# Hybrid attention/DeltaNet block with a 32-expert MoE: at each change of expert, the down of the old expert's last block is put ahead of the new expert's first gate_up

## Chip, cores and metric

The kernel runs on one core of one Trainium2 chip. The metric is device time of one execution in microseconds. The kernel before took 1259.33 us, the median of three runs (1258.27 to 1259.81).

## The reference

The function is one layer over 512 tokens of width 1024, all in float32. A first part (input projection, sliding-window attention, a gated DeltaNet, output projection) gives `h`; it is not touched here. Then comes the mixture of experts: each token goes to 4 of 32 experts, and each expert runs on its own tokens only.

```python
def clamped_swiglu_expert(xb, w_gu, b_gu, w_down, b_down):
    gu = xb @ w_gu + b_gu                      # (rows, 1024) @ (1024, 2048)
    gate = jnp.minimum(gu[:, :D_FF], SWIGLU_LIMIT)
    up = jnp.clip(gu[:, D_FF:], -SWIGLU_LIMIT, SWIGLU_LIMIT)
    act = (up + 1.0) * (gate * jax.nn.sigmoid(gate * SWIGLU_ALPHA))
    return act @ w_down + b_down               # (rows, 1024) @ (1024, 1024)
# y[token] += gate_of_row * clamped_swiglu_expert(row of the token); h = h + y
```

The weights of one expert are 8 MiB (`w_gu`) and 4 MiB (`w_down`).

## The kernel before

**Blocks.** The first part ends some 320 us into the span; everything after it is one loop over blocks. A block is 32 rows (token and gate) of one expert. With these inputs there are 81 blocks, numbered through over all experts. `LASTB[e]` holds the number of the last block of the e-th expert in the order of work; the expert with the fewest tokens' blocks comes last. The activations of a block are the stationary operand (32 columns), the weights stream through. The four column groups of the PE array work on four quarters of the output at once.

**PE** (L1102 to L1165). `gate_up(i)` multiplies block i, held transposed in XT, with the eight k slices of the gate/up weights into bank GPS; it waits for XT (`xt_ready`), for the bank (`gu_evac`), and at the first block of an expert for each of the four 2 MiB parts of the weights (`gu_in`). `down(i)` multiplies the activations of block i, held transposed in AT, with the down weights into DPS, half a PSUM bank. It waits for AT (`at_ready`), for DPS to be read by the block before (`yt_ready`), and for the two parts of the down weights. In program order the PE does gate_up(i), then down(i - 1), and so on; this holds inside an expert (`more_blocks`, L1134) and, before the change, at a change of expert too (`expert`, L1142). Each f32 matmul shows as two records in the trace, so a gate_up or a down has 64.

**DVE** (L1546 to L1632). `activate(i)` adds the bias to GPS (L1554), clamps (L1556, L1558), copies the next block's gathered tokens into XT (`x_turn`, L1549), multiplies with the sigmoid and the gate value (L1562, L1564), and transposes the result into AT (L1572). Before that transpose it spreads the down bias of block i - 1 into SIG (`spread_dn_bias`, L1580) and loads 16 token numbers into registers. After it, `y_evac(i - 1)` adds gate times down bias to DPS (L1585), transposes it into YTV (L1590) and adds 16 of its 32 columns onto the tokens in ACC (L1594). At a change of expert `spread_gu_bias` (L1438) spreads the new gate/up bias into BGU ahead of `activate`. For the last expert (`turn_first`) the spread and token loads come behind the transpose.

**ACT** (L669 to L697) does, in turn, the sigmoid of block i and the gathering of block i + 2 into XG. **POOL** (L424 to L454) does the other half of the gathering, of block i + 3 (L428), and then the other 16 adds of block i (L438).

**SP** (L340 to L350) issues the loads on one queue. There are two weight buffers; `reload` loads expert e + 2 into the buffer of expert e: first the four gate/up parts, each when the last gate_up of expert e has read it (L240); then it waits until the down bias of that expert's last block has been spread (`bdn_spread`, L344), loads the new biases (L231, L235) and then the two down parts, which wait for the last down of expert e (L246).

Of the kernel before, what the change touches and what calls it, by code (L numbers as in the profile page):

```python
# [25 lines left out]
HALF = BT // 2  # L26
# [13 lines left out]
def hybrid_block(nc, x, norm_mix_w, w_in, qn_w, kn_w, sinks, conv_w, a_log, dt_bias, out_norm_w, w_out,  # L40
                 norm_ffn_w, router_w, router_b, w_gu, b_gu, w_dn, b_dn, out):
    ctx = ExitStack()
    with ctx:
# [3 lines left out]
        def S_(name):  # L47
            if name not in sems:
                sems[name] = ctx.enter_context(nc.semaphore(name))
            return sems[name]  # L50
# [165 lines left out]
        def within(i, most, why):  # L216
            return i if isinstance(i, int) else nc.s_assert_within(i, 0, most, skip_runtime_bounds_check_because=why)
        def tokens_of(engine, i, first, count):
            at = within(i, MAXB, "no routing gives more than MAXB blocks, and one is gathered behind them")
            row = TOK[i:i + 1, first:first + count] if isinstance(i, int) else bass.at_runtime_partition(TOK[0:1, first:first + count], at)  # L220
            return nc.values_load_multi_w_load_instructions(row, engines=[engine], min_val=0, max_val=COLS - 1 if first < BT else S - 1,
                                                            skip_runtime_bounds_check_because="a token, or a column behind the last one")[1]
# [479 lines left out]
        def _(pe):  # L702
# [133 lines left out]
            for i in range(CHU + 2):  # L836
# [3 lines left out]
                if 2 <= i < NCH + 2:  # L840
# [7 lines left out]
                    v = AQ[0:k, (n - 1) // 2 if n else 0, 640:768] if n % 2 or n == 0 else AVS[:, n // 2 - 1, :]  # L848
# [253 lines left out]
            def gate_up(i, p, rnd, first_of_expert, first):  # L1102
                pe.wait_ge(S_("xt_ready"), i + 1)
                if not first:
                    pe.wait_ge(S_("gu_evac"), i)
                for k in range(KD):
                    if first_of_expert and k % 2 == 0:
                        pe.wait_ge(S_(f"gu_in{p}{k // 2}"), rnd)
                    for j in range(4):
                        rhs = GUW[p][:, k, :].rearrange("p (g n) -> p g n", g=2)[:, :, j * QW:(j + 1) * QW]  # L1110
                        last = pe.matmul(GPS[32 * j:32 * j + 32, :].rearrange("p (g n) -> p g n", g=2),  # L1111
                                         XT[:, 32 * k:32 * k + 32], rhs,
                                         start=(k == 0), stop=(k == KD - 1), tile_position=(0, 32 * j), skip_group_check=True)
                    if k % 2:
                        last.then_inc(S_(f"gu_read{k // 2}" if k < KD - 1 else "gu_ps"), 1)
                    if first and k in between:
                        between[k]()
            def down(i, p, rnd, to=DPS):
                pe.wait_ge(S_("at_ready"), i + 1)
                if to is DPS:  # L1120
                    pe.wait_ge(S_("yt_ready"), i + 1)
                pe.wait_ge(S_(f"dn_in{p}0"), rnd)
                for k in range(KD):
                    if k == KD // 2:
                        pe.wait_ge(S_(f"dn_in{p}1"), rnd)
                    for j in range(4):
                        rhs = DNW[p][:, k, :].rearrange("p (c q x) -> p q c x", c=KD, q=4)[:, j]
                        last = pe.matmul(to[32 * j:32 * j + 32, :].rearrange("p (c x) -> p c x", c=KD),  # L1128
                                         AT[:, 32 * k:32 * k + 32], rhs,
                                         start=(k == 0), stop=(k == KD - 1), tile_position=(0, 32 * j), skip_group_check=True)  # L1130
                    if k == KD // 2 - 1:
                        last.then_inc(S_("dn_read"), 1)
                last.then_inc(S_("d_ps"), 1)
            def more_blocks(e, p, before, rnd, last):  # L1134
# [5 lines left out]
                        down(i - 1, p, rnd)  # L1140
                return last
            def expert(e, p, before, rnd, prnd, last=None):  # L1142
                gate_up(before + 1, p, rnd, True, False)
                down(before, 1 - p, prnd)
                return more_blocks(e, p, before, rnd, last)
            gate_up(0, 0, 16, True, True)
            pe.wait_ge(S_("rows4"), 1)
# [30 lines left out]
        def _(v):  # L1178
# [255 lines left out]
            def spread_gu_bias(e, p, rnd):  # L1434
                v.wait_ge(S_(f"bias_in{p}"), rnd * 6)
                v.sem_inc(S_("passed"), 1)
                for q in range(4):
                    ins = v.stream_shuffle(BGU[:, QH * q:QH * q + QH], RAWP[p], [q] * 32)  # L1438
                ins.then_inc(S_("bias_spread"), 1)
                v.wait_ge(S_("bias_spread"), e + 1)  # L1440
# [105 lines left out]
            def x_turn(i):  # L1546
                v.wait_ge(S_("a_gathered"), i)
                v.wait_ge(S_("g_gathered"), i)
                v.tensor_copy(XT[:, :], XG[:, :]).then_inc(S_("xt_ready"), 1)  # L1549
            def activate(i, p, first, before_p=None, turn_first=False):  # L1550
                v.wait_ge(S_("gu_ps"), i + 1)
                if not first:
                    v.wait_ge(S_("at_ready"), i)
                tt(GU, GPS.rearrange("p (g n) -> p g n", g=2), BGU[:, :].rearrange("p (g n) -> p g n", g=2), ALU.add).then_inc(S_("gu_evac"), 1)  # L1554
                v.wait_ge(S_("gu_evac"), i + 1)
                ts(GATED, GATED, LIMIT, None, ALU.min).then_inc(S_("gate_ready"), 1)  # L1556
                x_turn(i + 1)
                ts(UP, UP, LIMIT, -LIMIT, ALU.min, ALU.max)  # L1558
                v.wait_ge(S_("sig_ready"), i + 1)
                if first:  # L1560
                    v.wait_ge(S_("lists_done"), 1)
                stt(out=SIG[:, :], in0=SIG[:, :], scalar=gate_of(i), in1=GATED, op0=ALU.mult, op1=ALU.mult).then_inc(S_("glu"), 1)  # L1562
                v.wait_ge(S_("glu"), i + 1)
                stt(out=GATED, in0=UP, scalar=1.0, in1=SIG[:, :], op0=ALU.add, op1=ALU.mult).then_inc(S_("act_ready"), 1)  # L1564
                v.wait_ge(S_("act_ready"), i + 1)
                def prepare():
                    spread_dn_bias(i - 1, before_p)
                    return tokens_of(v.engine, i - 1, 0, HALF)
                if not first and not turn_first:
                    toks = prepare()  # L1570
                v.wait_ge(S_("d_ps"), i + 1)
                v.transpose(ATV, ACTV).then_inc(S_("at_ready"), 1)  # L1572
                if turn_first:
                    toks = prepare()
                if not first:
                    y_evac(i - 1, toks)
            def spread_dn_bias(i, p):
                v.sem_inc(S_("passed"), 1)
                for h in range(2):
                    ins = v.stream_shuffle(SIG[:, QH * h:QH * h + QH], RAWP[p], [4 + h] * 32)  # L1580
                ins.then_inc(S_("bdn_spread"), 1)
                v.wait_ge(S_("bdn_spread"), i + 1)
            def y_evac(i, toks, start=DPS):
                v.wait_ge(S_("d_ps"), i + 2)
                stt(out=YG, in0=SIG[:, :], scalar=gate_of(i), in1=start, op0=ALU.mult, op1=ALU.add).then_inc(S_("y_ready"), 1)  # L1585
                v.wait_ge(S_("y_ready"), i + 1)
                if not (isinstance(i, int) and i == 0):
                    v.wait_ge(S_("g_added"), i)
                    v.wait_ge(S_("v_added"), i)
                v.transpose(YTV, YG.rearrange("p (k m) -> p k m", k=KD)).then_inc(S_("yt_ready"), 1)  # L1590
                v.wait_ge(S_("yt_ready"), i + 2)
                for m in range(len(toks)):
                    col = ACCV[:, :, bass.ds(toks[m], 1)]
                    ins = tt(col, col, YTV[:, :, m:m + 1], ALU.add)  # L1594
                ins.then_inc(S_("v_added"), 1)
# [9 lines left out]
            with v.If(last > 0):  # L1605
                activate(1, 0, False, 0)
# [2 lines left out]
                    activate(i, 0, False, 0)  # L1609
            def expert(e, p, before, rnd, last=None):  # L1610
                turn_first = last is not None
                spread_gu_bias(e, p, rnd)
                activate(before + 1, p, False, 1 - p, turn_first)
                if last is None:
                    last = v.value_load(LASTB[0:1, bass.ds(e, 1)], min_val=0, max_val=MAXB - 1)
                with v.If(last > before + 1):
                    with v.Fori(before + 2, last + 1) as i:
                        activate(i, p, False, p, turn_first)
                return last
# [31 lines left out]
```

## Time and profile before

| | |
|---|---|
| median of three runs | 1259.33 us |
| the profiled execution's own time | 1258.68 us |
| its span, first to last instruction | 1257.0 us |
| mean granted TensorE clock | 0.980 |
| PE matmul busy | 1180.9 us (94%) |
| DVE / ACT / POOL busy | 725.0 / 566.8 / 446.6 us |
| DMA | 427.71 MB, mean 340 GB/s |

Times are from one execution. A busy PE is a PE with a matmul under way by the profile, whose ends are modelled: two records that touch may overlap by some 0.2 us, so durations of gate_ups and downs are best read as the distance from start to start. The chain of work that ended last has PE with 65% of the span and DMA with 24%. `L1111` is the matmul of gate_up, `L1128` that of down.

### The profile page before, as it was taken

What the parts mean: (1) busy time and instruction counts of PE and PEld (TensorE: products, weight loads), DVE (VectorE), ACT (ScalarE), POOL (GpSimd) and SP (SyncE); (2) the same over time, 40 slices, a digit from 0 to 9 for tenths busy, and PEclk for the clock granted to TensorE, in tenths of its full rate; (3) what the DMA queues carried; (4) which work ended last, traced back from release to release, by engine and by line L of the source; (5) the groups of instructions that cost most, each with busy time, mean ns of one, the idle gap of its engine ahead of it and who ended that gap; (6) DMA issues with size and microseconds to landing.
All of it is one profiled execution on the core that took longest, in us unless ns stands there. A gap on an engine that the chain in (4) does not pass through costs nothing.

```text
span 1257.0 us, 46595 instructions
## 1 busy us (share of the span) xinstructions
PE 1180.9 (94%) x12074; PEld 554.9 (44%) x12075; DVE 725.0 (58%) x3048; ACT 566.8 (45%) x4249; POOL 446.6 (36%) x2632
## 2 busy tenths in 40 slices
PE   6999999999899998989998999999999778999996
PEld 5875456766444432323342444444444222334333
DVE  2237766555666664646565666666666444666564
ACT  3135666324354553535454555555555333555450
POOL 0000003000255553545454455555555333555451
PEclk9999999999999998999999999999999898999998
DMA  5141116347999999999999999999999999999995
GB/s 189 39 137 61 40 35 179 94 167 325 370 376 410 427 426 426 427 425 428 426 425 424 426 424 410 407 411 406 403 406 431 425 425 427 428 426 421 428 426 223
DMA packets 53768, 427.71 MB, mean 340 GB/s; under 512 B 13232, under 2 KB 25824, under 8 KB 29152
## 3 DMA queue, kind: packets, MB, share of 16 engines
q1 hardware_dynamic: 51552, 427.07, 82.5%
q10 hardware_dynamic: 2176, 0.13, 0.1%
q8 instruction: 22, 0.36, 0.1%
q14 instruction: 18, 0.15, 0.0%
HBM read 424.63 MB, written 2.36 MB: 340 GB/s over the span
## 4 chain that ended last, share of the span: by engine, by line
PE 65%; DMA 24%; DVE 5%; SPq 2%; issue 2%; ACT 1%; DVEq 0%; ACTq 0%; POOL 0%
PE PS L1111 30%; DMA W<-in_expert_w_gate_up 23%; PE PS L704 15%; PE PS L1128 14%; PE HTP L704 3%; SPq L231 1%; SPq L241 0%; DMA W<-in_norm_mix_w 0%; SPq L235 0%; PE HTP L880 0%; PE HTP L714 0%; DVE W L1192 0%; DVE ACC L1594 0%; PE HTP L1175 0%; DVE SIG L1580 0%
## 5 line engine op out<-in xcount | busy, mean ns | idle before, releaser
L1111 PE MATMUL PS<-W,XT 128*32 128x512 f32 x5184 | 594.5, 608 | 53.3 <-DMA W<-in_expert_w_gate_up 47.0
L1111 PEld LDWEIGHTS PS<-W,XT 128*32 128x32 f32 x5184 | 167.5, 111 | 426.3 <-issue 345.0
L673 ACT ACTIVATE XG<-HTP 128x6 f32 x2592 | 259.6, 181 | 155.3 <-issue 155.3
L428 POOL COPY XG<-HTS 128x2 f32 x1296 | 200.7, 213 | 298.3 <-DVE XT L1549 292.7
L438 POOL TENSOR_TENSOR ACC<-ACC 128x8 f32 x1292 | 226.9, 218 | 198.6 <-DVE ACC L1590 198.6
L1128 PE MATMUL PS<-W,AT 128*32 128x256 f32 x5120 | 293.5, 381 | 0.0
L1128 PEld LDWEIGHTS PS<-W,AT 128*32 128x32 f32 x5120 | 169.1, 111 | 149.2 <-issue 54.6
L704 PE MATMUL PS<-W 128*128 128x512 f32 (+3 forms) x680 | 219.3, 477 | 3.0 <-ACT W L625 1.1
L683 ACT ACTIVATE SIG<-GU 128x256 f32<-128x256 f32 x81 | 33.9, 418 | 339.1 <-DVE GU L1556 338.8
L1594 DVE TENSOR_TENSOR ACC<-ACC 128x8 f32 x1300 | 161.6, 187 | 13.8 <-issue 1.3
L704 PEld LDWEIGHTS PS<-W 128*128 128x128 f32 (+1 forms) x680 | 124.0, 191 | 76.8 <-issue 64.8
L676 ACT ACTIVATE XG<-HTS 128x2 f32 x1280 | 136.5, 192 | 0.2 <-issue 0.2
L1554 DVE TENSOR_TENSOR GU<-PS,BGU 128x512 f32<-128x512 f32 x81 | 56.0, 692 | 129.2 <-PE PS L1111 128.8
L1572 DVE STREAM_TRANSPOSE AT<-GU 128x256 f32<-128x256 f32 x81 | 53.1, 655 | 105.5 <-issue 97.9
L384 POOL TENSOR_TENSOR W<-W 128x512 f32<-128x512 f32 x4 | 5.1, 1266 | 190.8 <-ACT W L526 190.8
L1438 DVE LOAD_MASK_SELECT BGU<-RAW x128 | 1.8, 14 | 90.7 <-DMA RAW<-in_expert_b_down 73.9
L1562 DVE SCALAR_TENSOR_TENSOR SIG<-SIG,LATE,GU 128x256 f32<-128x256 f32 x81 | 39.3, 485 | 14.6 <-ACT SIG L683 14.6
L704 PE MATMUL HTP<-W 128*128 128x128 f32 (+6 forms) x368 | 43.5, 288 | 0.7 <-DMA W<-inv_scratch 0.6
L704 PEld LDWEIGHTS HTP<-W 128*128 128x128 f32 (+3 forms) x368 | 37.7, 186 | 12.7 <-issue 12.5
L1580 DVE STREAM_SHUFFLE SIG<-RAW 128x128 f32<-128x128 f32 x162 | 41.3, 300 | 0.7
L1590 DVE STREAM_TRANSPOSE ACC<-PS 128x256 f32<-128x256 f32 x81 | 36.4, 450 | 2.8
L1585 DVE SCALAR_TENSOR_TENSOR PS<-SIG,LATE,PS 128x256 f32<-128x256 f32 x80 | 35.9, 448 | 1.8 <-issue 1.8
(280 smaller groups left out, 630.9 us busy)
## 6 DMA issues: line engine op xcount, KB each, us to landing
W<-in_expert_w_gate_up SPq DMA_DIRECT2D x128, 2048.0 KB, 25.6
W<-in_expert_w_down SPq DMA_DIRECT2D x64, 2048.0 KB, 22.0
W<-in_w_in SPq DMA_DIRECT2D x10, 1024.0 KB, 5.9
W<-in_x SPq DMA_DIRECT2D x8, 512.0 KB, 11.1
W<-in_w_out SPq DMA_DIRECT2D x2, 1024.0 KB, 9.7
W<-in_w_out SPq DMA_DIRECT2D x1, 2048.0 KB, 8.2
RAW<-in_expert_b_gate_up SPq DMA_DIRECT2D x128, 2.0 KB
out<-W SPq DMA_DIRECT2D x8, 256.0 KB, 2.8
```

Of the source, the lines that this page charges most:

```text
L428: ins = g.tensor_copy(XGK[:, KP:KD, HALF + m:HALF + m + 1], HTS[:, :, bass.ds(toks[m], 1)])
L438: ins = g.tensor_tensor(col, col, YTV[:, :, m:m + 1], ALU.add)
L673: ins = a.activation(XGK[:, 0:KP, m:m + 1], HTP[:, :, bass.ds(toks[m], 1)], ACT.Copy)
L676: ins = a.activation(XGK[:, KP:KD, m:m + 1], HTS[:, :, bass.ds(toks[m], 1)], ACT.Copy)
L704: return pe.matmul(o, l, r, start=st, stop=sp_)
L1111: last = pe.matmul(GPS[32 * j:32 * j + 32, :].rearrange("p (g n) -> p g n", g=2), XT[:, 32 * k:32 * k + 32], rhs, start=(k == 0), stop=(k ...
L1128: last = pe.matmul(to[32 * j:32 * j + 32, :].rearrange("p (c x) -> p c x", c=KD), AT[:, 32 * k:32 * k + 32], rhs, start=(k == 0), stop=(k ...
L1554: tt(GU, GPS.rearrange("p (g n) -> p g n", g=2), BGU[:, :].rearrange("p (g n) -> p g n", g=2), ALU.add).then_inc(S_("gu_evac"), 1)
L1562: stt(out=SIG[:, :], in0=SIG[:, :], scalar=gate_of(i), in1=GATED, op0=ALU.mult, op1=ALU.mult).then_inc(S_("glu"), 1)
L1572: v.transpose(ATV, ACTV).then_inc(S_("at_ready"), 1)
L1580: ins = v.stream_shuffle(SIG[:, QH * h:QH * h + QH], RAWP[p], [4 + h] * 32)
L1594: ins = tt(col, col, YTV[:, :, m:m + 1], ALU.add)
```

## The change

On PE, `expert` calls down(before) ahead of gate_up(before + 1). On the DVE, `expert` does the spread of the old down bias, the token loads and y_evac of block `before` ahead of the new gate/up bias and of activate(before + 1), which gets `added=True` and leaves all three out. This holds for all 31 changes of expert, the last one included. Inside an expert nothing changes. No instruction is added to or taken from the work; ACT, POOL and SP keep their programs.

```diff
             def expert(e, p, before, rnd, prnd, last=None):
+                down(before, 1 - p, prnd)
                 gate_up(before + 1, p, rnd, True, False)
-                down(before, 1 - p, prnd)
                 return more_blocks(e, p, before, rnd, last)
...
-            def activate(i, p, first, before_p=None, turn_first=False):
+            def activate(i, p, first, before_p=None, turn_first=False, added=False):
...
                 def prepare():
                     spread_dn_bias(i - 1, before_p)
                     return tokens_of(v.engine, i - 1, 0, HALF)
-                if not first and not turn_first:
+                if not first and not turn_first and not added:
                     toks = prepare()
                 v.wait_ge(S_("d_ps"), i + 1)
                 v.transpose(ATV, ACTV).then_inc(S_("at_ready"), 1)
-                if turn_first:
+                if turn_first and not added:
                     toks = prepare()
-                if not first:
+                if not first and not added:
                     y_evac(i - 1, toks)
...
             def expert(e, p, before, rnd, last=None):
                 turn_first = last is not None
+                spread_dn_bias(before, 1 - p)
+                y_evac(before, tokens_of(v.engine, before, 0, HALF))
                 spread_gu_bias(e, p, rnd)
-                activate(before + 1, p, False, 1 - p, turn_first)
+                activate(before + 1, p, False, 1 - p, turn_first, True)
```

## Rows read from the trace of the kernel before

**Rows 1.** The page, part 2: busy tenths of PE and of the DMA engines, 40 slices.
```profile
PE   6999999999899998989998999999999778999996
...
DMA  5141116347999999999999999999999999999995
```

**Rows 2.** The page, part 5: groups; count | busy us, mean ns | idle before, releaser.
```profile
L1111 PE MATMUL PS<-W,XT 128*32 128x512 f32 x5184 | 594.5, 608 | 53.3 <-DMA W<-in_expert_w_gate_up 47.0
...
L1128 PE MATMUL PS<-W,AT 128*32 128x256 f32 x5120 | 293.5, 381 | 0.0
```

**Rows 3.** Waits of PE: who waited for whom, us in total, times, longest.
```profile
PE PS L1111 <- DMA W<-in_expert_w_gate_up: 47.0, 21, 3.1
...
PE PS L1111 <- issue: 3.6, 15, 0.6
```

**Rows 4.** Stretches: length, busy us (records) of PE, PEld, DVE, ACT, POOL; clock, DMA, GB/s.
```profile
332.00:470.00 138.00, 136.62 (x1680) 55.97 (x1680) 86.30 (x405) 71.19 (x665) 68.44 (x416) 1.00 0.96 404
...
693.00:955.00 262.00, 261.16 (x3236) 107.69 (x3232) 166.02 (x793) 131.46 (x1226) 132.47 (x800) 1.00 0.98 412
955.00:1057.00 102.00, 82.19 (x896) 28.42 (x892) 47.70 (x235) 36.70 (x344) 37.00 (x225) 0.90 1.01 427
```

**Rows 5.** Timeline, 742 to 770: start us, us, engine, line [idle before <-releaser].
```profile
748.68 7.05 PE L1111 MATMUL PS<-W,XT 128*32 128x512 f32 x64
...
755.55 3.64 PE L1128 MATMUL PS<-W,AT 128*32 128x256 f32 x64
...
759.42 7.07 PE L1111 MATMUL PS<-W,XT 128*32 128x512 f32 x64 [0.23 <-issue]
...
760.32 0.65 DVE L1572 STREAM_TRANSPOSE AT<-GU 128x256 f32<-128x256 f32 x1 [1.29 <-issue]
...
761.38 0.45 DVE L1590 STREAM_TRANSPOSE ACC<-PS 128x256 f32<-128x256 f32 x1
...
765.28 0.01 DVE L1438 LOAD_MASK_SELECT BGU<-RAW  x1 [1.35 <-issue]
...
766.30 3.64 PE L1128 MATMUL PS<-W,AT 128*32 128x256 f32 x64
...
767.58 0.29 DVE L1549 COPY XT<-XG 128x256 f32<-128x256 f32 x1
```

**Rows 6.** Timeline of SP: the closest two gate_up reloads.
```profile
933.04 1.90 SPq L241 DMA_DIRECT2D W<-in_expert_w_gate_up  x4
...
953.87 3.73 SPq L241 DMA_DIRECT2D W<-in_expert_w_gate_up  x4
```

**Rows 7.** Timeline, the start of gate_up 1.
```profile
332.64 0.29 DVE L1549 COPY XT<-XG 128x256 f32<-128x256 f32 x1 [0.38 <-ACT XG L673]
...
332.99 7.07 PE L1111 MATMUL PS<-W,XT 128*32 128x512 f32 x64 [1.58 <-DVE XT L1549]
```

**Rows 8.** Timeline, the last expert.
```profile
1220.00 3.64 PE L1111 MATMUL PS<-W,XT 128*32 128x512 f32 x32 [0.60 <-issue]
...
1233.85 3.63 PE L1128 MATMUL PS<-W,AT 128*32 128x256 f32 x64
...
1236.32 0.43 DVE L1564 SCALAR_TENSOR_TENSOR GU<-GU,SIG 128x256 f32<-128x256 f32 x1
...
1239.57 3.66 PE L1128 MATMUL HTP<-W,AT 128*32 128x256 f32 x64
...
1244.47 0.49 DVE L1585 SCALAR_TENSOR_TENSOR PS<-SIG,LATE,HTP 128x256 f32<-128x256 f32 x1 [0.22 <-DVE SIG L1580]
```

**Rows 9.** Timeline of PE: work behind three long waits.
```profile
595.45 3.48 PE L1111 MATMUL PS<-W,XT 128*32 128x512 f32 x16 [2.56 <-DMA W<-in_expert_w_gate_up]
...
685.12 1.92 PE L1111 MATMUL PS<-W,XT 128*32 128x512 f32 x16 [2.78 <-DMA W<-in_expert_w_gate_up]
...
1171.06 2.69 PE L1111 MATMUL PS<-W,XT 128*32 128x512 f32 x16 [2.63 <-DMA W<-in_expert_w_gate_up]
1173.51 4.62 PE L1128 MATMUL PS<-W,AT 128*32 128x256 f32 x64
```

## The prediction

> **What bounds the kernel now.** The slices of the page come first. From slice 11 on PE and the DMA engines are both mostly full (9s and a few 7s and 8s) [rows 1]. So the question is not which of the two is busier but whose waits end last. The groups of the page give the amount: 5184 matmuls are 81 gate_ups of 64 records, 5120 are 80 downs; the 81st down writes another bank [rows 2]. The waits of PE say that over the expert loop it stood 47.0 us for gate_up weights, in 21 waits, and nearly nothing else [rows 3]. The table of stretches shows how this alternates: between 693 and 955 PE is busy 261 of 262 us and the DMA moves 412 GB/s; between 955 and 1057 PE is busy 82 of 102 and the DMA is at its 427 [rows 4]. PE and DMA are thus nearly balanced: without its weight waits PE has little to give away.
>
> **The unit of the sum.** In a full stretch a gate_up goes from one start to the next down in 6.87 us (748.68 to 755.55) and a down takes 3.45 us (its record shows a modelled end 0.2 later); where a pair of experts starts, 0.42 us comes on top (759.42 less 755.55 is 3.87), 15 times [rows 3, 5]. SP's gate_up reloads are released by the last gate_up of an expert. The closest two are 20.8 us apart, two blocks (20.64), so every expert but the last has two or more blocks; the last has one, block 80, whose gate_up starts at 1220.00 [rows 6, 8]. There are 31 changes of expert.
>
> From the start of gate_up 1 (332.99) to that of the last down (1239.57) pass 906.6 us [rows 7, 8]. In it are 80 x 6.87 = 549.6, 80 x 3.45 = 276.0, 15 x 0.42 = 6.3 and 5.7 from the last gate_up's end to the last down (1233.85 to 1239.57): 837.6. The other 69.0 are the 47.0 of weight waits and 22.0, which I put down to matmuls at half clock behind them.
>
> **What moves, part by part.** Call b the last block of the old expert and G the end of its gate_up.
>
> *Down ahead of gate_up, on PE.* Now down(b-1) covers the DVE chain of b, and gate_up(b+1) covers the rest, so down(b) never waits. Afterwards down(b) comes straight behind down(b-1), and it needs two things of the DVE: the turned activations (L1572) and the y of b-1 turned out of DPS (L1590). Both stand in one unchanged piece of code. For G = 755.55 that L1590 ends at 761.83; down(b-1) ends at G + 3.45 = 759.00 [rows 5]. The last DVE write to the PE start takes 0.06 us (L1549 ends at 332.93, the gate_up that waits for it starts at 332.99) [rows 7]. So PE stands 761.89 - 759.00 = **2.89 us, 31 times: 89.6**. The 0.42 of a new pair now lies ahead of this down, inside its wait: 6.3 less. Of it 1.29 are the token loads ahead of the turn (the idle "issue" before L1572) [rows 5]; the change drops them only from the first block of an expert, and that one is never the last here.
>
> *Second wait.* The down used to stand between gate_up(b+1) and gate_up(b+2). Now gate_up(b+2) follows at once and needs L1554 (the bank) and L1549 (XT) of b+1. At a first gate_up of an expert L1549 ends at 767.87, 1.57 after the gate_up's end at 766.30; with the 0.06 this is **1.63 us, 30 times (the last expert has one block): 48.9** [rows 5]. The one place of the trace with this order, gate_up 0 to gate_up 1, shows 1.58 [rows 7].
>
> *Last expert.* Its down waited 5.72 us after its gate_up, for down(before), spread and turn. Now L1564 ends 2.90 after the gate_up, the turn takes 0.65 and follows at once: 3.65 with the hand-overs. And the last y_evac (L1585 at 1244.47) no longer stands behind 16 adds of the block before: 1.1 less [rows 8].
>
> *On the DVE*, what goes ahead of activate(b+1) is the spread, 16 token loads, L1585, L1590, 16 adds, then the four shuffles of the gate_up bias. The adds of b-1 end 1.35 before the next work at 765.28 (G + 9.7); 0.6 for the spread, 1.3 for the loads, 3.1 for L1585 to L1594 (L1572 ends at 760.97, the adds at 763.93) and 1.1 for four shuffles (twice the spread's two) give G + 15.8. gate_up(b+1) ends at G + 3.45 + 2.89 + 3.45 + 6.87 = G + 16.7 [rows 5]. The cover is 0.9 us; I take 0. If it is gone, it is L1554 and with it gate_up(b+2) that come late, us for us.
>
> *POOL and ACT.* POOL's 16 adds of b stay behind gather(b+3), which waits for XT of activate(b+1); they take as long as now, and nobody needs them until y_evac(b+1), a gate_up and a down later. ACT's gathers keep their releases. Nothing.
>
> *SP.* It waits for the down spread before it issues the biases and the down weights. The spread ends 3.5 after the gate_up of its activate (L1572 less the loads is 759.03), so at G + 3.45 + 6.87 + 3.5 = G + 13.8 [rows 5]; it will end at G + 10.2, and down(b) ends 4 us earlier: down weights leave about 3.5 us sooner. That mends the 404 and 412 GB/s of two stretches: 138 x (1 - 404/427) + 262 x (1 - 412/427) = 16.6 us of DMA time at most [rows 4]. It is worth time only if the DMA still bounds. An expert's six parts of 2048 KB take 12.58 MB / 427 = 29.5 us of the DMA; PE took 81/32 x 10.32 = 26.1 and will take 30.6. PE becomes the bound, and its 47.0 of waits with the 22.0 behind them go.
>
> Without the clock: 549.6 + 276.0 + 89.6 + 48.9 + 3.65 = 967.8 against 906.6, and 1.1 less at the end: **+60 us**.
>
> **The clock.** This is the disputed term. Ten waits of PE lie between 2.56 and 3.15 us. Behind eight of them the granted clock fell to half (1.2 GHz of 2.4): behind 2.56 us of idleness the quarter of a gate_up took 3.48 instead of 1.92, behind 2.63 us it took 2.69 and the down 4.62 instead of 3.64; behind those at 685.12 (2.78) and 1016.78 it stayed [rows 9]. The 2.89 stalls are of this kind, those of 1.63 are not: no wait that short, alone, was followed by a fall. One fall costs 1.56 to 1.75 us. The bounds are none (0) and all (31 x 1.75 = 54); I take the share seen, 8 of 10, so 25 x 1.65 = **41 us**. The Trainium skill, "TensorE: Matmul & The Clock Gate", section "Why this matters for your kernels", advises no idle gaps above about 3 us between bursts. By that rule a stall of 2.9 leaves the clock whole, and the sum would end at +60; the rows at 595 and 1171 speak against it.
>
> Sum: +60 + 41 = +101 on the profiled run's 1258.68: **1360 us**. That run lies 0.65 under the median of 1259.33, which I leave out.
>
> **Rivals.**
> 1. *The clock holds.* +60: 1319 us. For it: PE is fully busy before and after each stall, while several of the eight falls had a second wait near. Against: 595 and 1171. 0.20.
> 2. *The DVE comes late at the first gate_up of an expert.* The 0.9 us of cover rests on one 1.35 us of loop overhead and a chain without a gap. If it is 1.9 longer, 1 us x 30 comes on top: 1390 us. 0.12.
> 3. *Faster.* The stalls fall where PE waits for weights anyway, and the DMA stays the bound, now without gaps. The point that decides: PE has 69.0 to lose over 31 changes, 2.2 us each; below this the end is set by the DMA, 16.6 us earlier at best: 1242 us. It needs down(b) ready almost as down(b-1) ends. Against it, L1590 alone ends 2.83 after that. 0.02.
> 4. *Nothing.* The stalls use up just the waits, or the order in effect does not change: 1259 us. The code's waits exclude nearly all of it. 0.02.
>
> My forecast (PE-bound, clock lost at most stalls) has 0.64. All slower cases make 0.96. A difference under 0.2% (2.5 us) could not be told from none here.
>
> **Range.** Low end: rival 1 with stalls 0.2 and 0.1 shorter (9 us): 1310. High end: all 31 falls at 1.75 (+13) and 0.4 us of DVE lateness at each change (+13): 1387. Left out are most of rival 2 and the last two.
>
> **What would show it.** In the changed profile, L1128 after a change of expert should wait for DVE L1590, 31 times about 2.7 to 2.9 us; L1111 30 times about 1.5 for L1549; waits for gate_up weights should be nearly gone and the DMA's GB/s lower. Falls of the clock should be counted near 25. I am wrong if PE still waits over 20 us for weights, if the stall at down is under 2 us, or if L1554 starts more than 0.5 after the end of its gate_up.

## The result

The changed kernel took 1368.07 us (median of four runs, 1366.11 to 1371.11), the kernel before 1258.8 (four runs, 1258.13 to 1259.81). The ratio is 1.086, with a 95% interval of 1.0836 to 1.0884: 109 us slower. The forecast was 1360 us in a range of 1310 to 1387. The profiled execution of the changed kernel took 1369.76 us, its span is 1368.0.

### The profile after

First the page of the changed kernel: the head, the busy tenths of PE and of the DMA engines, and the two groups of matmuls.

```profile
span 1368.0 us, 46670 instructions
...
PE   7999999998889788888888988898888888888886
...
DMA  5121045079898999989879677777899999979981
...
L1111 PE MATMUL PS<-W,XT 128*32 128x512 f32 x5184 | 572.7, 593 | 44.6 <-DVE XT L1549 43.4
L1128 PE MATMUL PS<-W,AT 128*32 128x256 f32 x5120 | 336.7, 422 | 88.4 <-DVE ACC L1590 46.7
```

Against [rows 1, 2] the counts are the same; it is the idle time ahead of them that changed its owner. Ahead of gate_ups stood the DMA with 47.0 us, now it is the DVE with 43.4; ahead of downs stood nothing, now 88.4. The 9s of the DMA have given way to 6s to 8s in the long experts. gate_up records are shorter than before (593 ns against 608) and down records longer (422 against 381): half clock used to fall on gate_ups behind weight waits, now it falls on downs.

The waits of PE, the counterpart of [rows 3] (who waited for whom, us in total, times, longest):

```profile
PE PS L1128 <- DVE ACC L1590: 46.7, 16, 3.1
PE PS L1111 <- DVE XT L1549: 43.4, 31, 1.6
PE PS L1128 <- DVE AT L1572: 41.6, 15, 3.0
...
PE HTP L1128 <- DVE AT L1572: 2.6, 1, 2.6
```

That is the new loop: 31 stalls at a down and 31 at a gate_up, of which one (gate_up 1) was there before. There is no row for weights any more.

The stretches of [rows 4] (length, busy us with records of PE, PEld, DVE, ACT, POOL, then clock, DMA share, GB/s):

```profile
332.00:470.00 138.00, 119.68 (x1361) 47.98 (x1357) 70.71 (x336) 60.10 (x563) 55.53 (x341) 0.95 0.91 382
...
693.00:955.00 262.00, 232.42 (x2719) 94.90 (x2712) 141.48 (x682) 112.83 (x1059) 112.17 (x681) 0.96 0.81 339
955.00:1057.00 102.00, 86.44 (x1028) 36.34 (x1024) 54.10 (x263) 42.20 (x395) 43.27 (x264) 0.95 0.95 401
```

Between 693 and 955 the clock was 1.00 and is 0.96, and the DMA went from 412 to 339 GB/s. PE waits for no weights in any of them: PE, with its stalls behind the DVE, sets the pace.

One change of expert on PE, the counterpart of [rows 5] (start us, us, engine, line, tiles, idle before and its releaser):

```profile
770.90 3.64 PE L1128 MATMUL PS<-W,AT 128*32 128x256 f32 x64
777.28 5.35 PE L1128 MATMUL PS<-W,AT 128*32 128x256 f32 x64 [2.74 <-DVE AT L1572]
782.41 7.08 PE L1111 MATMUL PS<-W,XT 128*32 128x512 f32 x64
...
503.01 3.66 PE L1128 MATMUL PS<-W,AT 128*32 128x256 f32 x64 [2.76 <-DVE AT L1572]
```

down(b-1) starts at 770.90 and would be done at 774.35; down(b) starts at 777.28, 2.93 later, and takes 5.35 us in place of 3.66. The row at 503.01 is one of the four of 31 where it kept its 3.66 after a stall of the same length. The granted clock in both (columns as above) says why:

```profile
777.60:780.80 3.20, 3.20 (x36) 1.97 (x32) 2.17 (x19) 1.61 (x16) 2.63 (x15) 0.50 1.02 435
503.10:506.40 3.30, 3.30 (x64) 2.42 (x67) 2.42 (x20) 1.83 (x19) 2.87 (x16) 1.00 1.04 442
```

And the DVE beside the change at 777.28:

```profile
775.68 0.64 DVE L1572 STREAM_TRANSPOSE AT<-GU 128x256 f32<-128x256 f32 x1 [1.28 <-issue]
...
776.73 0.45 DVE L1590 STREAM_TRANSPOSE ACC<-PS 128x256 f32<-128x256 f32 x1
...
782.78 0.49 DVE L1585 SCALAR_TENSOR_TENSOR PS<-SIG,LATE,PS 128x256 f32<-128x256 f32 x1 [2.86 <-PE PS L1128]
...
786.68 0.30 DVE L1438 STREAM_SHUFFLE BGU<-RAW 128x128 f32<-128x128 f32 x1
...
789.60 0.69 DVE L1554 TENSOR_TENSOR GU<-PS,BGU 128x512 f32<-128x512 f32 x1 [2.62 <-issue]
```

L1590 ends at 777.18 and the down starts 0.10 later. (The profile names L1572 as releaser at half of the changes; the start follows L1590 by 0.10 at these too. At the 15 changes where a new pair of experts starts it follows L1590 by 0.23 to 0.30.) The first L1554 of the new expert starts 0.32 after its gate_up's end at 789.28, having been free for 2.6 us: the DVE is not late.

### The profile page after: what moved, and what is told of

The parts are those of the page before. It is cut to its first block, busy times and chain, and to the rows that moved or that the text cites. A ratio compares the mean times of both kernels' runs of the same rounds, so it can differ in the third digit from the quotient of the medians.

```text
span 1368.0 us, 46670 instructions
## 1 busy us (share of the span) xinstructions
PE 1212.7 (89%) x12074; PEld 584.3 (43%) x12075; DVE 727.1 (53%) x3048; ACT 566.6 (41%) x4249; POOL 443.5 (32%) x2632
## 4 chain that ended last, share of the span: by engine, by line
PE 69%; DVE 14%; issue 9%; DVEq 3%; ACT 2%; DMA 1%; ACTq 0%; SPq 0%; POOL 0%
PE PS L1111 34%; PE PS L1128 16%; PE PS L704 13%; DVE GU L1554 3%; PE HTP L704 3%; DVEq L221 3%; DVE SIG L1580 1%; DVE BGU L1438 1%; DVE SIG L1562 1%; DVE GU L1564 1%; ACT SIG L683 1%; DVE AT L1572 1%; DVE GU L1556 1%; DVE XT L1549 1%; DVE ACC L1590 1%
## 5 line engine op out<-in xcount | busy, mean ns | idle before, releaser
L1111 PE MATMUL PS<-W,XT 128*32 128x512 f32 x5184 | 572.7, 593 | 44.6 <-DVE XT L1549 43.4
L1128 PE MATMUL PS<-W,AT 128*32 128x256 f32 x5120 | 336.7, 422 | 88.4 <-DVE ACC L1590 46.7
L1111 PEld LDWEIGHTS PS<-W,XT 128*32 128x32 f32 x5184 | 172.4, 110 | 411.5 <-issue 331.6
L1128 PEld LDWEIGHTS PS<-W,AT 128*32 128x32 f32 x5120 | 191.4, 121 | 245.6 <-issue 118.2
L438 POOL TENSOR_TENSOR ACC<-ACC 128x8 f32 x1292 | 223.8, 217 | 147.3 <-DVE ACC L1590 127.4
L1554 DVE TENSOR_TENSOR GU<-PS,BGU 128x512 f32<-128x512 f32 x81 | 56.0, 692 | 275.0 <-PE PS L1111 199.1
L1572 DVE STREAM_TRANSPOSE AT<-GU 128x256 f32<-128x256 f32 x81 | 52.4, 647 | 66.3 <-issue 64.0
L1585 DVE SCALAR_TENSOR_TENSOR PS<-SIG,LATE,PS 128x256 f32<-128x256 f32 x80 | 37.1, 464 | 68.1 <-PE PS L1128 65.1
L704 PE MATMUL HTP<-W 128*128 128x128 f32 (+6 forms) x368 | 43.4, 288 | 0.8 <-DMA W<-inv_scratch 0.7
L1590 DVE STREAM_TRANSPOSE ACC<-PS 128x256 f32<-128x256 f32 x81 | 36.4, 450 | 2.8
L1564 DVE SCALAR_TENSOR_TENSOR GU<-GU,SIG 128x256 f32<-128x256 f32 x81 | 34.4, 425 | 2.8
```

The source lines that it names most:

```text
L438: ins = g.tensor_tensor(col, col, YTV[:, :, m:m + 1], ALU.add)
L704: return pe.matmul(o, l, r, start=st, stop=sp_)
```

## The experiments

They ran in two groups, each on one chip beside the kernel before. Its median was 1258.85 in the first (early loads, filled stall, 16 of 31 changes, the queue) and 1259.83 in the second (the control, the transposes, the XT copy first, both edits); between the groups that 1.0 us is to be kept in mind.

### Shorter DVE chain at the stall

```diff
+                early = not first and not turn_first and not added
+                if early:
+                    toks = tokens_of(v.engine, i - 1, 0, HALF)
                 v.wait_ge(S_("gu_ps"), i + 1)
...
-                if not first and not turn_first and not added:
-                    toks = prepare()
+                if early:
+                    spread_dn_bias(i - 1, before_p)
```

> The changed kernel, with the 16 token loads of the DVE's y_evac taken ahead of its wait for the gate_up, so that the chain from the end of a gate_up to L1572 and L1590 is 1.29 us shorter. My theory (the down stall is this DVE chain, and a stall near 3 us costs a fall of the clock besides): the stall at the down goes from 3.0 to 1.7 us (31 x 1.29 = 40 us), the 27 falls vanish (27 x 1.69 = 46 us), and the weight waits come back a little, since an expert now takes the PE about as long as the DMA: 1283 to 1292 us. Rival A (the falls follow the change of order, not the length of the stall): 1328 us, with some 27 falls. Rival B (down(b) waits for something else, the bank or the DMA): no change, 1368 us.

Measured: 1295.87 us, ratio 1.0275 (1.0225 to 1.0324). PE's waits, and one change:

```profile
PE PS L1128 <- DVE ACC L1593: 29.7, 16, 1.9
PE PS L1128 <- DVE AT L1575: 26.0, 15, 1.7
...
PE PS L1111 <- DMA W<-in_expert_w_gate_up: 1.1, 1, 1.1
```

```profile
739.06 3.64 PE L1128 MATMUL PS<-W,AT 128*32 128x256 f32 x64
744.43 3.66 PE L1128 MATMUL PS<-W,AT 128*32 128x256 f32 x64 [1.73 <-DVE AT L1575]
```

The stalls shrank and with them every slow down went: all 31 took 3.66, and the mean clock of the run is 0.997. That kills both rivals. My own number was 4 us low at its upper end, since the stall is 1.92 (744.43 less 739.06 and 3.45), and 2.05 where a new pair of experts starts, not 1.7. The DVE row that shows the new limit:

```profile
742.84 0.64 DVE L1575 STREAM_TRANSPOSE AT<-GU 128x256 f32<-128x256 f32 x1 [0.27 <-PE PS L1128]
```

The transpose (L1575 here is L1572) now waits for down(b-1) to be done with AT, of which there is one. Once the chain is short, the order itself holds the stall: turn into AT, L1585, L1590, one after the other behind down(b-1). A second AT and a second DPS were not tried, nor a down that waits for L1585 alone: DPS and the YG that L1590 reads share a PSUM bank. The Trainium skill, "PSUM — Partial Sum Buffer", section "PSUM bank collisions raise a hardware error", rules out a PE write beside a DVE read of one bank; no run here shows it.

### The same loads early in the old order

The same edit on the kernel before, as a control.

> The kernel before with the same early token loads as in the run e1_loads_early. My theory (in the old order the DVE chain is covered by the gate_up that stands ahead of the down, so its length is worth nothing): 1257 to 1261 us, no difference from before. Rival (the chain limits the kernel in the old order too, and part of what that run gained has nothing to do with the new order): up to 1.0 us for each of 80 blocks less, bounded by the DMA at about 1245 us.

Measured: 1260.12 us, ratio 1.0005 (0.9995 to 1.0015). The chain is worth nothing in the old order; what it cost in the new one is the price of the new order.

### The stall filled with work

```diff
             def expert(e, p, before, rnd, prnd, last=None):
+                pe.wait_ge(S_("gu_evac"), before + 1)
+                for _ in range(9):
+                    mm(GPS[:, 0:P], ident[:, :], ident[:, :], True, True)
                 down(before, 1 - p, prnd)
```

> The changed kernel, with nine 128x128 f32 matmuls of the identity by itself into the free gate_up bank inside the stall ahead of the down at each change of expert (about 2 us of work of no use). My theory: the stalls themselves stay, the PE is no longer idle in them, the clock stays whole at all 31, and the time falls by 27 x 1.69 = 46 us to 1322 us. Rival (the slow downs come from something else than the idle time before them, such as cold reads of the new operand, or these matmuls do not count): 1366 to 1370 us, with the down behind the stall still at 5.35 us.

Measured: 1327.37 us, ratio 1.0551 (1.0487 to 1.0615), one change of it:

```profile
752.44 3.64 PE L1129 MATMUL PS<-W,AT 128*32 128x256 f32 x64
756.01 2.27 PE L705 MATMUL PS<-ident 128*128 128x128 f32 x18
758.82 3.66 PE L1129 MATMUL PS<-W,AT 128*32 128x256 f32 x64 [0.54 <-issue]
762.27 7.08 PE L1112 MATMUL PS<-W,XT 128*32 128x512 f32 x64
```

From start to start the two downs are 6.38 us apart, in the changed kernel 6.38 (770.90 to 777.28): the stall is as long as it was, only not idle, and the down behind it takes 3.66. All 31 did, and over all 31 the stalls sum to 94.2 us, against 94.1. So the clock alone was worth 45.4 us in the loop. The run was 41 us faster and not 45 (and 5 slower than I expected), because the last change took some back. Here is the very last down, first in the changed kernel, then in this run:

```profile
1351.70 3.66 PE L1128 MATMUL HTP<-W,AT 128*32 128x256 f32 x64 [2.58 <-DVE AT L1572]
...
1307.66 5.35 PE L1129 MATMUL HTP<-W,AT 128*32 128x256 f32 x64 [3.87 <-DVE AT L1576]
```

In this run it waited 1.3 us longer and was itself slow, which is another 1.7.

With 18 transposes in place of the nine matmuls:

> As the run e2_filled_stall, but the stall is filled by 18 transposes of the identity in place of the nine matmuls, the same 2 us of PE work. Theory 1 (a transpose keeps the clock as a matmul does): 1326 to 1328 us, one fall or none in the loop. Theory 2 (transposes do not count as work for the clock, as a page of the Trainium skill has it, TensorE: Matmul & The Clock Gate, Part 4): some 27 falls, 1366 to 1370 us.

Measured: 1326.98 us, ratio 1.0536 (1.0518 to 1.0554), mean clock 0.997. For the clock a transpose was as good as a matmul here.

### The new order at 16 of 31 changes

```diff
             def expert(e, p, before, rnd, prnd, last=None):
-                down(before, 1 - p, prnd)
+                if p:
+                    down(before, 1 - p, prnd)
                 gate_up(before + 1, p, rnd, True, False)
+                if not p:
+                    down(before, 1 - p, prnd)
```

The DVE's part likewise.

> The order is changed only at the 16 changes into odd experts; at the 15 into even ones the kernel is as before. Theory 1, mine (PE had 69 us of waits for weights and of slow matmuls behind them to lose before any stall costs time): 16 stalls of 3.1 + 1.6 us with 1.7 of clock are 102 us, of which a good half goes into waits that vanish; 1285 to 1296 us. Theory 2 (each change of order costs its share, the effect is linear): half of 109, 1313 us. Theory 3 (the DMA hides all of it): 1259 us.

Measured: 1289.41 us, ratio 1.0229 (1.018 to 1.0277). 

```profile
PE PS L1128 <- DVE ACC L1593: 46.5, 16, 3.1
PE PS L1111 <- DVE XT L1552: 22.6, 16, 1.6
...
PE PS L1111 <- DMA W<-in_expert_w_gate_up: 5.0, 2, 2.5
```

Half of the changes cost 31 us, 28% of the 109 of all. Slow downs followed 15 of the 16 stalls. The first stalls eat the waits for weights (47.0 have become 5.0), and the other 15 changes cost 79 us. That is theory 1, and it refutes an equal price per change.

### The second stall

```diff
+                if added:
+                    x_turn(i + 1)
                 tt(GU, GPS.rearrange("p (g n) -> p g n", g=2), BGU[:, :]...
...
-                x_turn(i + 1)
+                if not added:
+                    x_turn(i + 1)
```

> The changed kernel, but at the first block of an expert the DVE copies XT (L1549) ahead of the bias add (L1554), so that both are done 0.3 us sooner after the gate_up. My theory (the second stall, ahead of the next gate_up, is bound by these two): it goes from 1.59 to about 1.3 us at 30 changes, and the time falls by 9 us to 1359 us. Rival (what the second stall costs is made up elsewhere, or it is bound by the gathers of ACT and POOL): 1366 to 1370 us.

Measured: 1355.36 us, ratio 1.0766 (1.0731 to 1.0801).

```profile
PE PS L1111 <- DVE GU L1556: 34.7, 30, 1.2
```

The second stall went from 43.4 less one 1.6 to 34.7, 7 us, and it does lie on the path. The rest of the 12.7 us goes with the clock: 22 of the downs behind a stall were slow in this profile, 27 in the one of the changed kernel, and five at 1.68 are 8 us; the last expert, whose down waited 1.5 us longer here and was slow, takes some of that back. Whether the shorter second stall has a part in the fewer falls stays open. Both edits together:

> Both edits, the early token loads and the XT copy first, on the changed kernel: as near as the new order gets without new buffers. The down stall stays at the 1.9 us of the run e1_loads_early (L1572 now waits for down(b-1) to be done with AT, and the down for L1590), the second at 1.3: 9 us less than that run's 1296, of which the weight waits take back 0 to 4, so 1287 to 1291 us. Rival (the DMA already bounds that run): 1294 to 1297 us.

Measured: 1291.55 us, ratio 1.0258 (1.0241 to 1.0275), 4 us under the run with the early loads alone, where I had expected 9 less 0 to 4, and half a microsecond above the expected range. The second stall shrank by 0.24 us, not by 0.3 (34.8 us for 30 of them in this profile), and weight waits of 2.5 took a part back. It stays 32 us behind the kernel before. No version with the new order came nearer to the old one than 30 us.

### The down part of the queue alone

```diff
                 gu_part(e, p, range(4), through)
+                dn_part(e, p, [0], through)
                 sp.wait_ge(S_("bdn_spread"), through)
                 gu_bias(e, p)
                 dn_bias(e, p)
-                dn_part(e, p, range(2), through)
+                dn_part(e, p, [1], through)
```

on the kernel before.

> The kernel before, but SP loads the first down part as soon as the last down of the old expert has read it, ahead of its wait for the spread of the down bias; biases and the second part behind. This does alone what the change did for the DMA queue on the side: down weights leave earlier. My theory: where PE sets the pace the queue ran dry for a few us per expert, 16.6 us in all at most, and the DMA sets the end: 1250 to 1256 us. Rival (PE sets the pace in those stretches and the gaps of the queue cost nothing): 1259 us. Rival 2 (the gate_up bias now lands 5 us later and holds up the DVE at each change where the weights are awaited): 1262 to 1270 us.

Measured: 1260.5 us, ratio 1.0014 (0.9988 to 1.0039). My theory did not come true. PE's waits, and two of the stretches:

```profile
PE PS L1112 <- DMA W<-in_expert_w_gate_up: 27.6, 13, 3.0
PE PS L1112 <- DVE XT L1550: 21.9, 9, 3.3
```

```profile
332.00:470.00 138.00, 136.76 (x1684) 55.90 (x1688) 85.63 (x404) 70.24 (x655) 68.04 (x416) 1.00 0.99 414
...
693.00:955.00 262.00, 257.83 (x3152) 104.83 (x3148) 165.60 (x797) 131.03 (x1225) 131.59 (x800) 0.99 0.98 410
```

The long stretch moves 410 GB/s where it moved 412 [rows 4], though down weights leave early. Where PE works without a gap, an expert of three blocks of 10.32 us takes 12.58 MB from the queue, and that is 406 GB/s: the rate in this stretch is PE's pace, not a queue that ran dry. In the stretch from 332 to 470 the rate did rise, from 404 to 414 GB/s, and the run was no faster for it. The second rival is there as well: the gate_up bias now lands behind 2 MiB more, and the XT copy behind the bias is late eight times. (The ninth is the 1.6 us at gate_up 1, which the kernel before has too.) 27.6 + 20.3 = 47.9 us stand in the place of 47.0. Which of the two rivals decided was not separated: waits for weights did shrink by 19.4 us, and waits for the late bias took their place.

## Why the prediction was right, and where it was off

From the start of gate_up 1 to that of the last down 1017.1 us pass (334.62 to 1351.70) where 906.6 did. By the terms of the sum:

| term | predicted | measured |
|---|---|---|
| stall ahead of down(b), 31 | 89.6 | 94.1 |
| stall ahead of gate_up(b+2), 30 | 48.9 | 47.6 |
| slow downs, falls of the clock | 41 (25 x 1.65) | 45.4 (27, 1.68 each) |
| last gate_up's end to last down (5.7 before) | 3.65 | 3.59 |
| waits for weights, and what followed them | -69.0 | -69.0 |
| new pair of experts, 15 x 0.42 | -6.3 | -6.3 |
| tail behind the last down | -1.1 | -1.1 |

The measured column sums the distances from start to start of the trace that the rows above sample. With 80 gate_ups and 80 downs at 6.87 and 3.45 it closes to 0.8 us. The -69.0 and the -6.3 are not read off rows of their own: the list of waits holds no wait for weights any more, and the sum closes with them.

The sum gave +101 us, the two profiled spans differ by 111. The range was right and the mechanism too; the 10 us are the stall (4.5), the slow downs (4.4) and 1.6 ahead of gate_up 1, less 1.3 for the smaller second stall, and the 0.8 that the table leaves.

**Balanced PE and DMA.** Right: the 69 us of slack went, and the run with half of the changes shows that it went first.

**The down stall.** Right in mechanism, place and nearly in size. The DVE chain ends at G + 6.28 as read; the hand-over is 0.10, not 0.06, and at each new pair of experts it is 0.23 to 0.30, which I put down to the start of the loop over pairs. That is 4.5 us.

**The second stall.** Right: 1.59 for 1.63.

**The clock.** It was the disputed term, and the share of 8 in 10 was a little low: 27 of 31. Rival 1, the clock that holds, would have given 1319; with the idle time filled the kernel takes 1327. The advice of the Trainium skill, "TensorE: Matmul & The Clock Gate", section "Why this matters for your kernels", to avoid gaps above about 3 us is no safe side here: stalls whose idle time the trace gives as 2.7 to 3.1 lost the clock in most cases, and of the 15 that were under 3.0 from end to start (by 3.45 us a down) 12 did. I looked only at waits of 2.56 us and more when I priced this. The kernel before has a shorter one with a fall behind it, a wait of 2.09 us with one of 0.60 ahead of it; the second row is the stretch that follows, with the granted clock:

```profile
1225.73 2.75 PE L1111 MATMUL PS<-W,XT 128*32 128x512 f32 x16 [2.09 <-DMA W<-in_expert_w_gate_up]
...
1226.80:1230.00 3.20, 1.68 (x8) 0.00 (x0) 0.00 (x0) 0.00 (x0) 0.00 (x0) 0.50 1.01 423
```

Such a quarter of a gate_up takes 1.92 us at full clock.

**The DVE's cover.** I counted 0.9 us; it was 2.3 (from the last bias shuffle's end at 787.0 to 789.28), mainly because the 1.35 of "issue" ahead of the bias shuffles shrank to about 0.1. The slow down adds only some 0.3: it delays the gate_up by 1.7, but L1585 waits for that same down. Behind the down at 503.01, which kept its clock, the cover was 2.0. Rival 2 did not come true at these changes. At the last change there was no cover: in the changed kernel the last shuffle ends 0.1 after the gate_up. In the five runs whose down there kept its clock, PE then waited 3.8 to 4.1 us for the last turn, not 2.6, and the last down was slow.

**The queue.** Wrong, in the step on SP and in the price of rival 3. Down weights did leave sooner (SP waited 267.1 us for the spread, 368.9 before), and in the old order it was worth nothing. The larger part of the 16.6 us that I took for DMA time to be won, the 9.2 of the long stretch, is the pace of PE; a faster kernel at 1242 was not to be had that way. Whether earlier down weights without the later bias would bring anything was not tried. The forecast did not rest on it.

**The rest.** 1.6 us of the profiled run lie ahead of gate_up 1, in code that the change does not touch (334.62 against 332.99); the run with both edits started it at 332.23, so this is chance.

## What to carry to other kernels

A software pipeline that puts a product one step behind its operand's preparation is worth the length of that preparation: before taking it out at a seam, read from the trace how long after its last input the operand is ready, and subtract what still runs in between. Where two resources are balanced, the first stalls are free and the rest are paid in full, so half of a change can cost much less than half. And a stall of PE should be priced with the clock that it may cost behind it: here 1.7 us on a stall of 3.0, all of it gone once the stall was 1.9 or was filled with matmuls of no use.

## What the runs showed of the hardware

- Stalls with 2.7 to 3.1 us of idle PE (by the profile) were followed by half clock in 27 of 31 cases, 1.68 us of loss each. The share moves from kernel to kernel: 22 of 31 with the XT copy first, 15 of 16 with the order changed at 16 changes. Stalls with 1.4 to 1.9 us of idle PE were followed by none in 61 (run with early loads). Behind a weight wait of 2.09 us in the kernel before the clock did fall. What sets the stalls that kept the clock apart from those of the same length that lost it stays open.
- Transposes kept the clock whole as well as matmuls: 1326.98 against 1327.37 us, mean clock 0.997 against 0.996. The Trainium skill, "TensorE: Matmul & The Clock Gate", section "Part 4: PE-mode transpose", says that a transpose does not count as PE-busy in the same way; for filling a stall of this length the measurement decides against it.
